# Block sums, bit search and gate products in a two-block transformer kernel: three edits to the order of work

## What is computed

```python
rel = jax.nn.relu(jnp.einsum('bqhd,bsd->bqhs', qib, kif))        # 4 index heads of 64
iscore = jnp.einsum('bqhs,bqh->bqs', rel, wib * w_scale)
iscore = jnp.where(visible[None], iscore, -jnp.inf)
_, idx = lax.top_k(iscore, 256)
...
merged = sigmoid(g_ssm) * (y_ssm @ w_proj_ssm) + sigmoid(g_att) * (y_att @ w_proj_attn)
```

## Time and profile before

| | |
|---|---|
| median of 3 runs | 4071.26 us (4070.88 to 4079.56) |
| the profiled execution | 4065.74 us, span 4064.0 |
| PE busy | 3706.5 us, 91% |
| DVE busy | 2568.9 us, 63% |
| ACT busy | 1831.5 us, 45% |
| POOL busy | 1332.7 us, 33% |
| mean granted PE clock | 0.955 |
| masks_and_gates | about 248 to 477 us |
| swiglu_up | about 1034 to 1474 us |

### The profile page before, as it was taken

One profiled execution on the slowest core, in us unless ns is written; L12 is line 12 of the kernel. 1 busy time (PEld: TensorE's weight loads), 2 busy tenths in 40 slices (PEclk: granted clock), 3 DMA queues, 4 the chain that ended last, 5 costly groups with the idle time before them and its releaser, 6 DMA issues. The chain is left out here.

```text
span 4064.0 us, 53206 instructions
## 1 busy us (share of the span) xinstructions
PE 3706.5 (91%) x19688; PEld 3141.5 (77%) x19688; DVE 2568.9 (63%) x4283; ACT 1831.5 (45%) x3365; POOL 1332.7 (33%) x1223
## 2 busy tenths in 40 slices
PE   7889777798999999999999987879999999999888
PEld 6667656577777778878887786768799999999867
DVE  6569783425566666613376577867567776776666
ACT  3135555504333334521344356764555455555444
POOL 1423220033443310211234461100366666666400
PEclk9979888899999999999999998989999999999989
DMA  4222301354376674532134585756311111111064
GB/s 151 82 78 82 118 14 37 122 193 149 114 236 226 233 262 158 161 133 70 55 121 154 179 195 108 147 160 200 91 40 53 37 48 47 40 50 42 22 220 147
DMA packets 348286, 485.37 MB, mean 119 GB/s; under 512 B 45355, under 2 KB 218956, under 8 KB 344044
## 3 DMA queue, kind: packets, MB, share of 16 engines
q1 hardware_dynamic: 311116, 371.33, 29.0%
q0 software_dynamic: 34608, 106.45, 9.0%
q10 hardware_dynamic: 2304, 4.20, 0.3%
HBM read 337.43 MB, written 144.47 MB: 119 GB/s over the span
## 5 line engine op out<-in xcount | busy, mean ns | idle before, releaser
L119 PE MATMUL hg_acc<-l_first_ws,l_XT 128*128 128x256 f32 x2880 | 359.6, 284 | 0.0
L119 PEld LDWEIGHTS hg_acc<-l_first_ws,l_XT 128*128 128x128 f32 x2880 | 348.8, 192 | 0.0
L119 PE MATMUL hg_acc<-l_XT,hg_ws 128*128 128x512 f32 x1440 | 342.9, 394 | 0.0
L119 PEld LDWEIGHTS hg_acc<-l_XT,hg_ws 128*128 128x128 f32 x1440 | 266.6, 188 | 52.4
L4619 POOL TENSOR_TENSOR hg_DD<-hg_BB 128x256 f32<-128x256 f32 x224 | 174.4, 778 | 258.4 <-PE hg_pA L4378 132.5
L4476 DVE TENSOR_TENSOR hg_DD<-hg_Q,hg_DD 128x256 f32<-128x256 f32 x224 | 205.1, 916 | 73.7 <-ACT hg_DD L4547 73.6
L119 PE MATMUL even_bank<-l_first_ws,l_XT 128*128 128x512 f32 x888 | 206.2, 390 | 3.2 <-PEq L852 1.9
L119 PE MATMUL even_bank<-even_ws,l_XT 128*128 128x512 f32 x876 | 204.4, 390 | 0.0
L119 PEld LDWEIGHTS even_bank<-l_first_ws,l_XT 128*128 128x128 f32 x888 | 166.2, 188 | 40.7 <-issue 6.0
L119 PEld LDWEIGHTS even_bank<-even_ws,l_XT 128*128 128x128 f32 x876 | 163.9, 188 | 34.0
L119 PE MATMUL am_g_acc<-l_XT,am_ws 128*128 128x512 f32 x768 | 179.1, 396 | 8.6 <-ACT am_stage L2064 8.6
(11 more groups left out here) (739 smaller groups left out, 9547.1 us busy)
## 6 DMA issues: line engine op xcount, KB each, us to landing
l_first_raw<-in_odd_w_in SPq DMA_DIRECT2D x64, 512.0 KB, 5.3
l_first_raw<-in_even_w_in SPq DMA_DIRECT2D x16, 1024.0 KB, 5.3
l_room_tiles<-hidden SPq DMA_DIRECT2D x63, 256.0 KB, 8.5
da_first_X<-q_k_hi POOLq DMA_DIRECT2D x24, 512.0 KB, 8.0
da_first_X<-q_k_lo POOLq DMA_DIRECT2D x24, 512.0 KB, 13.7
l_room_tiles<-y_even SPq DMA_DIRECT2D x45, 256.0 KB, 8.3
ffn_y<-in_w_ffn_down SPq DMA_DIRECT2D x22, 512.0 KB, 4.7
weight_sums_w_ffn_down<-ffn_y SPq DMA_DIRECT2D x11, 1024.0 KB, 5.1
```

The source lines that it names most:

```text
L119: mm = pe.matmul(out, lhs(p, k), rhs(q, k), start=start and i == 0, stop=stop and i == n - 1, skip_group_check=skip)
```

## The change

In swiglu_up the four differences of a block sum become single steps (`block_sum(b, q)`). The steps of a chunk, four or eight, are divided over five places, behind the operand's split of P6, P5, P7, P4 and P3. Each step now counts on the semaphore, so the store waits for four.

In masks_and_gates the search keeps the value in the form in which it is compared: the probe is the value with one bit flipped, so the separate `trial` and `flip` words and one small operation a round go. The first two gate groups are computed in 16 pieces (one k-tile, three matmuls), one behind each of the last 16 score steps. POOL splits weight chunk 1 after hiding the third block's keys. `evicted_after` starts two groups higher.

```diff
-                    sp.wait_ge(b_made, 3 * (b + 1))
+                    sp.wait_ge(b_made, 4 * (b + 1))
...
+                def block_sum(b, q):
+
+                    b11, b12, b21, b22 = (room[b % 2][:, r, :] for r in range(4))
+                    if q == 0:
+                        dve.wait_ge(b_ld[b % 2], (b // 2 + 1) * 2 * DMA)
+                        dve.tensor_tensor(b11, b12, b11, ALU.subtract).then_inc(b_made, 1)
+                    if q == 1:
+                        dve.tensor_tensor(b12, b12, b22, ALU.subtract).then_inc(b_made, 1)
+                    if q == 2:
+                        dve.wait_ge(b_made, 4 * b + 1)
+                        dve.tensor_tensor(b22, b22, b11, ALU.subtract).then_inc(b_made, 1)
+                    if q == 3:
+                        dve.wait_ge(b_made, 4 * b + 3)
+                        dve.tensor_tensor(b21, b21, b22, ALU.subtract).then_inc(b_made, 1)
...
                     if name == "P4":
                         dve.wait_ge(gate0_out, c + 1)
                         dve.tensor_tensor(gate0[:, :], x, gate0[:, :], ALU.mult).then_inc(h0, 1)
-                        for b in blocks_at.get(c, [])[:1]:
-                            block_sums(b)
                     if name == "P3":
-                        for b in blocks_at.get(c, [])[1:]:
-                            block_sums(b)
...
                     if i + R < len(order):
                         split_operand(i + R)
+                    todo = [(b, q) for b in blocks_at.get(c, []) for q in range(4)]
+                    turn_of = ("P6", "P5", "P7", "P4", "P3").index(name) if name in ("P6", "P5", "P7", "P4", "P3") else None
+                    if turn_of is not None:
+                        for b, q in todo[len(todo) * turn_of // 5:len(todo) * (turn_of + 1) // 5]:
+                            block_sum(b, q)
...
-    CW, G, B = 2 * P, 4, 4
+    CW, G, B, EARLY = 2 * P, 4, 4, 2
...
-        return max(0, min(chunks * G, int((4.1 * (i + 1) + 3) / 5.5)))
+        return max(0, min(chunks * G, int((4.1 * (i + 1) + 14) / 5.5)))
...
+                pieces = [(g, k) for g in range(EARLY) for k in range(KD)]
+                steps = range(NB * I_H - len(pieces), NB * I_H)
+
+                def piece(g, k):
+                    mm = split_product(pe, g_acc[:, g, :], lambda p, q: ws[:, 0, p, q, g // 2 * P:(g // 2 + 1) * P],
+                                       lambda p, q: XT[:, p, q, g % 2 * NC:(g % 2 + 1) * NC], [k], start=k == 0, stop=k == KD - 1,
+                                       skip=True)
+                    if k == KD - 1:
+                        mm.then_inc(summed, 1)
+
...
                         mm.then_inc(ready, 1)
+                        if i in steps:
+                            if i == steps[0]:
+                                pe.wait_ge(split, 1)
+                            piece(*pieces[i - steps[0]])
                 for c in range(chunks):
                     s = c % 2
                     pe.wait_ge(split, c + 1)
-                    for g in range(G):
+                    for g in range(EARLY if c == 0 else 0, G):
...
                     if i == 0:
-                        dve.tensor_copy(probe, trial).then_inc(probed, 1)
+                        dve.tensor_copy(probe, value).then_inc(probed, 1)
                     else:
-                        link(dve.tensor_tensor(trial, value, bits[:, i - 1:i].to_broadcast([P, NB]), ALU.bitwise_or))
-                        dve.tensor_tensor(probe, trial, flip, ALU.bitwise_xor).then_inc(probed, 1)
+                        dve.tensor_tensor(probe, value, bits[:, i - 1:i].to_broadcast([P, NB]), ALU.bitwise_xor).then_inc(probed, 1)
...
                     if i == 0:
-                        link(dve.tensor_copy(flip, minus))
-                        link(dve.copy_predicated(flip, enough, plus))
+                        link(dve.tensor_copy(value, minus))
+                        link(dve.copy_predicated(value, enough, plus))
                     else:
-                        link(dve.copy_predicated(value, enough, trial))
-                link(dve.tensor_tensor(flip, flip, plus, ALU.bitwise_xor))
-                link(dve.tensor_tensor(level, value, flip, ALU.bitwise_xor))
+                        link(dve.copy_predicated(value, enough, probe))
+                link(dve.tensor_tensor(level, value, plus, ALU.bitwise_xor))
...
                                        channel_multiplier=1).then_inc(hid, 1)
-                for c in range(1, chunks):
+                    if b == NB - 4:
+                        split_chunk(1)
+                for c in range(2, chunks):
                     split_chunk(c)
```

More of the change, by code:

```diff
@@ L1969, in masks_and_gates @@
         const = pl.sb("const", [P, NCONST], U32)
-        word = pl.sb("word", [P, 6, NB], U32)
+        word = pl.sb("word", [P, 4, NB], U32)
         count = pl.sb("count", [P, 4, NB])
@@ L1978, in masks_and_gates @@
         least = const[:, SEARCH_BITS + 2 * NB:].bitcast(F32)
-        value, flip, trial, probe, enough, level = (word[:, i, :] for i in range(6))
+        value, probe, enough, level = (word[:, i, :] for i in range(4))
         found, above, rest, lowest = (count[:, i, :] for i in range(4))
```

## The result

The changed kernel takes 4090.85 us (median of 5 runs, 4086.18 to 4092.98) against 4070.88 us before in the same series: ratio 1.0048, 95% interval 1.0032 to 1.0063. The forecast was 4074.6 with a range to 4086.

The account below looks back on a forecast made before the run. The prediction took PE to bound the up stage and DVE's chain to set the end of masks_and_gates. Terms of +2.3 and +1.0 us gave +3.3: 4069.0 for the profiled execution, 4074.6 for the median, range 4057 to 4086.

Parts of the forecast that it names:

- I let it rise near 265.5: Score steps: PE's clock goes from half to full near 265.5; 7.4 us at half clock cost 3.7 more.
- Rival (b): Clock stays at half speed through the score steps: rising at 280 adds 7.3 us, never before the search 17; chance 0.12.
- What unshared steps cost: Last 16 score steps, each running alone on PE: 52 records of 512 columns, 23.8 us; 34.7 with the pieces.
- The hand-overs: Changes between score steps and gate pieces on PE: 0 to 3 us, taken 0.8.
- The search: masks_and_gates: one small piece fewer a round, 6.4 us off; POOL's hold-ups 3 off; ACT's wait 0.7 on.
- Split of chunk 1 in its new place: POOL's split behind the third block's scores: costed at nothing, 6.5 us if uncovered; 3.0 us off the search.
- Who ends the stage: masks_and_gates still ends with DVE's chain, 2 us later, with PE done near 462.
- The term at P4 of the last chunk: End of the up stage: last quarter of the sum made later, +3.4 us (0 to 4); PE's wait near 4.7.
- The term of the loop: Up stage, 17 chunks with spread sums: weights settle about 3 us late, -2.4 us, between -19.8 and +3.
- the store's landing of 8.56 us: Up stage, SP's queue: the next load waits 8.56 us for the store, with the weights behind it.
- Rival (a): Up stage loses its waits: -14 us in all, 4057, or half of it, 4065; chance 0.30 with its half.
- Level: Whole kernel: median of three runs 5.52 us above the profiled execution; the same difference added to the forecast.

Follow-up runs that it names:

- e2: Kernel before plus only the 16 gate pieces, one behind each of the last 16 score steps: 4115.59 us, ratio 1.0120.
- c1: Kernel before with all 24 score steps on rows 0 to 63, so no two share PE's rows, no pieces: 4087.03 us, ratio 1.0043.
- c4: Kernel before with all 16 gate pieces in a row ahead of the ninth score step: 4078.35 us, ratio 1.0028.
- e1: Changed kernel without the gate pieces between score steps, eviction quota as before: 4043.6 us, ratio 0.9942 to the kernel before.
- e3: Kernel before with only the block sums spread as in the change: 4059.12 us, ratio 0.9979.
- s2: Kernel before with block sums spread as single steps, but each ahead of the operand's split: 4049.51 us, ratio 0.9955.
- s1: Kernel before with block sums still whole, but moved behind the operand's split: 4104.65 us, ratio 1.0093.
- e4: Kernel before with only the search of three small pieces a round: 4060.13 us, ratio 0.9981.
- s3: Kernel before with only SP's order changed, both stores of a chunk ahead of both loads: 4060.19 us, ratio 0.9977.
- m2: e1 with POOL's split timed to the search rounds and the quota at 3.6 us a round: 4041.49 us, ratio 0.9928 to the kernel before.
- c3: Kernel before with eight gate pieces, one behind each of the last eight score steps: 4092.25 us, ratio 1.0058.

## Why the prediction was wrong

**The clock.** The step that failed is "I let it rise near 265.5". It rose at 333.8, and the scores ended 48.4 us later than before instead of 14.9. The rows said that small score matmuls had not lifted it for 8 us; I took the 128-row pieces as a reason against, though the rise before came in a stretch in which two steps shared the rows, and the edit ends just that. The Trainium skill, page TensorE: Matmul & The Clock Gate, Part 1, has activity release the clock; PE was busy 46.00 of 46.00 us at 0.50 in e2, so being busy did not do it here, and the measurement decides.

**The price of the rival.** Rival (b) named the right place and mechanism and said 17 us for "never before the search". Its rule, half a us for each us of later rise, is sound. The fault is the time up to which it was taken: 300, where the search would start at full clock, though the slow clock moves that start as well. By my own terms the 16 steps and pieces take 2 x (23.8 + 10.9) = 69.4 us at half clock, so they end near 327.5, and (327.5 - 265.5) / 2 is +31 instead of +17. That would have put the range's end over 4100. The stretch from the ninth step to the first product behind the last measured 72.8 us (258.77 to 331.54).

**What unshared steps cost** was nearly right: 23.8 us at full clock for 16 steps is 47.6 at half, and c1 has 44.5 (start +21.7). The hand-overs were the term too small, 0.8 us taken. In the rows above a piece takes 1.58 us (320.97 to 322.55), where three products in a row at half clock take 3 x 0.427 = 1.28 (the pitch in c4 from 263.64 on); a step of 1024 columns takes 3.71 (317.26 to 320.97), where four records in c1 take 4 x 0.853 = 3.41. That is 0.30 us for each change at half clock. The sum comes out: 44.5 for the steps, 19.2 for 15 pieces and 31 changes make 73.0, against 72.8 measured. My sum had counted 16 pieces, but the last one stands behind the last step and holds up no score. The Trainium skill, page TensorEngine Tiling (Array Packing), Key Properties, says that a change of tiling mode drains TensorE; the trace agrees in that each change costs time. That it is a drain isn't shown.

**The search** was right: 11.4 us shorter, expected 10.1 behind the first probe. Small pieces -6.6 (6.4), the six locks 27.6 to 22.0, -5.6 (3), chunk 1's lock -1.6 (1.4), ACT's wait +2.4 (0.7). Each lock now costs 3.66, one piece at 3.83 in place of 0.17. Start: beside the +48.4 of the steps, DVE's lag and the copy give 2.1 back (2.6 expected).

**Split of chunk 1 in its new place** cost nothing, though it did prolong one DVE multiplication (L2130) to 3.65 us at 278.61: PE's steps of that block kept coming every 4.43 us. **Who ends the stage** was right (DVE), but "PE has 6.5 us to spare" took PE's end as fixed; it moved with the rounds, as e1 showed.

**The up stage.** -9.9 instead of +1.0. The term at P4 of the last chunk was right in kind, 2.6 instead of 3.4 (an idle time of 3.91, 4.7 expected; from start to start of the matmuls around it 4.29, the 4.3 of e3's expectation). The term of the loop was -13.1 instead of -2.4; the other 0.6 lies outside both. The step that failed is the store's landing of 8.56 us, taken from the earlier trace rows as a property of the store. That store was issued right behind a load, as this row of before shows, which stands just ahead of the store at 1109.39:

```profile
1108.53 0.81 SPq L1428 DMA_DIRECT2D ffn_y<-in_w_ffn_down  x2
```

Before, eight stores left 0.5 to 0.8 us behind a load, and the next load followed them after 7.9 to 8.6 us; behind the others it followed after 3.9 to 5.2. In the changed kernel no store of the loop leaves less than 2.2 us behind a load, and the next load goes out after 3.8 to 6.2 us. Whether the slow store waited in the queue or shared the bandwidth with the load isn't separated. So the loop that I walked through does not settle at weights 3 us late with PE waiting; ACT still waits 3.02 us for them at 1174.66, but silu and copy come early enough now. Rival (a) was mostly true, and s2 makes it true whole.

**Level.** I added 5.5 us for the median against the profiled execution. In the changed kernel the median is 2.1 us below the profiled execution, so the difference is +27 between profiled executions and +20 between medians. The moment of the rise may be a part of this: the last score matmul starts 33.8 to 34.6 us behind the first where the clock rose at 268 to 270 (the profiled executions of before, e1 and s1), 38.3 where it rose at 279 to 282 (those of e3, e4, s2, s3, m2). The profiled execution of before was of the early kind, 4.5 us ahead in its start, and the changed kernel has no rise there that could come early or late. But the profiled executions of e4, s2 and m2 are of the late kind and yet the fastest of their kernels, so the cause of the level stays open.

## What to carry to other kernels

Before you put work between two instructions of PE, look whether they overlap: what stands between two matmuls on different rows takes away their sharing and, as here, with it the clock. Price a slower clock as work times two; a price per us of later rise is right only if the end of the work moves with the clock. A DMA's latency read right behind another DMA belongs to the two together; before you build a loop on it, find the same transfer alone.

## What the runs showed of the hardware

PE busy 100% does not mean full clock: 46 us without a gap at 0.50 with 64-row steps that run alone, three 128-row products between each two (e2), and 33 us with such steps only (c1). With pairs on both halves it rose while the scores ran, with or without products between the pairs (12 profiles, 15.6 to 33.0 us behind the first score matmul; what sets the moment is open). When 128-row products alone ran it rose within 2.3 to 4.4 us of their start (the changed kernel, e2, c1, c3).

A change between a 64-row step and a 128-row product cost 0.30 us at half clock, 31 times 9 us.

POOL's subtraction holds up DVE's two-input pieces of 6 elements (3.83 us for 0.17), but not DVE's counting: 96.4 us for 128 passes with six locks in e1 and 96.4 in m2. The number of inputs is not all of it. The COPY of the earlier trace rows, which reads one tensor, took 1.77 us during POOL's rounding of chunk 1 (285.74 to 287.63), and the multiplication at 278.61, which reads one tensor and a word per row, took 3.65. The Trainium skill, page GPSIMD Engine Reference, section Specifications, names contention with DVE instructions in a 2-port perf mode or with two SBUF inputs; the pieces with two inputs agree, and no run here shows which mode the COPY and the multiplication ran in. Placed beside the counting, POOL's work was nearly free: one piece of 1.88 us was left.
